# Three host-unrolled head loops of an attention stage written as hardware loops on ScalarE, VectorE and TensorE

## The chip, the cores and the metric

The kernel is a Bass program for one core of a Trainium2 chip. Each engine (TensorE = PE, VectorE = DVE, ScalarE = ACT, GpSimd = POOL, SyncE = SP) has an instruction stream of its own, written by hand, and the streams meet only in semaphores. The metric is the device time of one execution in microseconds.

## The reference, cut to what matters

Two transformer blocks run one after the other on 1024 tokens of width 1024. The first has a short convolution, dilated attention and an FFN. The second puts 16 meta tokens ahead (1040 rows), runs two attention branches A and B over them, merges these with gates, and ends in an expert-choice FFN of 16 experts. The change lies in branch A, the differential attention of 8 heads. Each head has two score maps (m = 0, 1) of width 64 and one value matrix of width 128:

```python
A_HEADS, A_HEAD_DIM = 8, 64
def diff_attention(q, k, v, pos, slopes, lam):
    # q, k: [B, L, H, 2, d]; v: [B, L, H, 2d]
    scale = A_HEAD_DIM ** -0.5
    k_meta = pos < N_META
    def block(qb, pb):
        qp = pb[0]
        s = jnp.einsum('bqhmd,bkhmd->bhmqk', qb, k).astype(jnp.float32) * scale
        dist = jnp.abs(qp[:, None] - pos[None, :]).astype(jnp.float32)
        dist = jnp.where((qp[:, None] < N_META) | k_meta[None, :], 0.0, dist)
        s = s - slopes[None, :, None, None, None] * dist
        p = jax.nn.softmax(s, axis=-1)
        w = p[:, :, 0] - lam * p[:, :, 1]
        return jnp.einsum('bhqk,bkhe->bqhe', w.astype(v.dtype), v)
    return sweep_queries(block, q, pos[None])
```

q, k and v of each head are columns of one projection of the normed rows, h @ w_in.

## The kernel before, in words

All arithmetic is float32. A projection (`project_split`, L513) splits both operands into a rounded part and a remainder and adds three products, so each weight tile of 1024x128 takes three passes on PE. SP loads the tiles one after the other into two buffers, POOL splits them (L540).

Branch A goes head by head. A head has nine query tiles, `t` = 0 to 8: eight of 128 rows and one of 16 (the meta rows). For each tile PE makes the scores of tile `t + 1` (`scores`, L2050), DVE adds the bias and finds the row extremum for both maps (`scores`, L1668), ACT takes both exponentials (`exp`, L1374), DVE combines the two maps into one (`combine`, L1684), PE transposes the result (`turn_probs`, L511), ACT copies the transposes out of PSUM (`take_pt_meta`, `take_pt`, L1382 and L1387), and PE multiplies them with the values (`values`, L2083 and L2084); ACT scales the product into `o_tok` (`result`, L1393). Between these pieces PE projects q, k and v of the next head, one ninth per tile in two halves (`unit`, L2019, 24 matmuls a tile), and ACT and DVE take them out of PSUM (L1351, L1360, L1631, L1635). At tile 5 and at the last tile PE and DVE also make the scores of the 16 meta keys for the next head (`meta_scores`, L2032, L1644, L1648).

The functions `head(h, odd)` of ACT (L1405 on), DVE and PE write one head each. Two heads make a pair because the buffers alternate with the parity of the head. Head 0 and head 7 are written apart. Heads 1 to 6 are three pairs, written in `for i in range((HEADS - 2) // 2)` on ACT (L1443), DVE (L1718) and PE (L2136); with HEADS = 8 this is Python's own loop over i = 0, 1, 2, so the program holds all six heads in a row, and every wait compares with a constant. POOL (L1266) already has a hardware loop over the same pairs. Other stages have hardware loops (`Fori`) on all engines: the first block's attention (L1002 on PE, L820 on DVE, L679 on ACT), the gates and branches (L2190), the first three heads of each group in branch B (L2309; its fourth head is written apart, with the same function), and the experts (L2419).

What sets the order around the change is the written order alone. At the border between two heads PE has: the values of tile 7, the meta scores of the next head, then the scores of tile 1 of the next head, the transpose of its values' meta rows (L511 on `vTa`), and the next projection unit.

Of the kernel before, what the change touches and what calls it, by code (L numbers as in the profile page):

```python
# [38 lines left out]
HEADS = 8  # L39
# [78 lines left out]
def build(nc, A, out):  # L118

    ctx = ExitStack()  # L120
    with ctx:
# [1045 lines left out]
        with nc.Block() as block:  # L1167
# [170 lines left out]
            def _(act):  # L1338
# [64 lines left out]
                def head(h, odd, first=False, last=False):  # L1403

                    for t in range(NT + 1):  # L1405
                        par = (odd + t) % 2
                        before = (h, t - 2) if t >= 2 else None if first else (h - 1, NT + 1 + t - 2)
                        if before:
                            result(*before)
                        if t == 0:  # L1410
                            act.wait_ge(S["aa_v"], 3 * h + 1)
                            act.activation(Va_meta[odd][0:META, :], bank(6, P, 0, META), ACT.Copy).then_inc(S["aa_vs"], 1)
                        after = (h, odd, t + 1) if t < NT else None if last else (h + 1, 1 - odd, 0)
                        if after:
                            exp(after[0], (after[1] + after[2]) % 2, after[2], 0)
                        if before:
                            square(*before)
                        take_pt_meta(h, par, t, first and t < 2)
                        if after:
                            exp(after[0], (after[1] + after[2]) % 2, after[2], 1)  # L1420
                        take_pt(h, par, t)
                        if not last:
                            kind, c = UNITS[t]
                            unit_done(h + 1, kind, c)
                            take_unit(h + 1, 1 - odd, kind, c, WEAVE)
                        if t == 0:
                            for n in range(2):
                                act.wait_ge(S["aa_v"], 3 * h + n + 2)
                                act.activation(Va[:, 4 * n:4 * n + 4, :], bank(5 + n).rearrange("p (t n) -> p t n", n=P), ACT.Copy).then_inc(S["aa_vs"], 1)
# [10 lines left out]
                for c in range(3):  # L1440
                    take_values(0, c, (6, 7, 4)[c])
                head(0, 0, first=True)
                for i in range((HEADS - 2) // 2):  # L1443
                    head(2 * i + 1, 1)
                    head(2 * i + 2, 0)
                head(HEADS - 1, 1, last=True)
# [161 lines left out]
            def _(dve):  # L1608
# [82 lines left out]
                def head(h, odd, first=False, last=False):  # L1691

                    for t in range(NT + 1):
                        if t < NT:
                            attend(h, (odd + t + 1) % 2, t + 1, first)
                        elif not last:
                            attend(h + 1, 1 - odd, 0)
                        if last:
                            continue
                        kind, c = UNITS[t]  # L1700
                        if kind == "k":
                            lower_keys(h + 1, 1 - odd, c, WEAVE)
                        elif kind == "q":
                            lower_queries(h + 1, c)
                        if t == 5:
                            meta_scores(h + 1, True)
                        elif t == NT:
                            meta_scores(h + 1, False)
# [6 lines left out]
                attend(0, 0, 0, True)  # L1715
                meta_scores(0, False)
                head(0, 0, first=True)
                for i in range((HEADS - 2) // 2):  # L1718
                    head(2 * i + 1, 1)
                    head(2 * i + 2, 0)  # L1720
                head(HEADS - 1, 1, last=True)
# [29 lines left out]
                for g in range(KV):  # L1751
                    z0 = g * (GROUP + 1)
                    for n in range(GROUP + 1):
                        i = z0 + n
# [245 lines left out]
            def _(pe):  # L2000
# [85 lines left out]
                def head(h, odd, first=False):  # L2086

                    for t in range(NT + 1):
                        if t < NT:
                            scores(h, odd, t + 1, first)  # L2090
                        else:
                            scores(h + 1, 1 - odd, 0)
                        if t == 0:
                            pe.wait_ge(S["aa_vf"], 3 * h + 3)
                            if not first:
                                pe.wait_ge(S["aa_pt"], 18 * h)
                            turn(bank(6, P, 0, META), vTa[:, T1:T2]).then_inc(S["aa_v"], 1)
                        kind, c = UNITS[t]
                        unit(h + 1, 1 - odd, kind, c, 0)
                        turn_probs(h, (odd + t) % 2, t, first)  # L2100
                        unit(h + 1, 1 - odd, kind, c, 1)
                        if t >= 1:
                            values(h, odd, t - 1, 18 * h + 2 * t + 1)
                        else:
                            if not first:
                                values(h - 1, 1 - odd, NT, 18 * h + 1)
                            pe.wait_ge(S["aa_pt"], 18 * h + 2)
                            turn_values(h)
                        if t == 5:
                            pe.wait_ge(S["aa_pt"], 18 * h + 2 * t + 2)  # L2110
                            meta_scores(h + 1, True)
                        elif t == NT:
                            pe.wait_ge(S["aa_pt"], 18 * h + 2 * t + 2)
                            meta_scores(h + 1, False)
# [18 lines left out]
                pe.wait_ge(S["aa_qs"], 3)  # L2133
                project_split(pe, 0, A0 + 2, (6, 7, 4), CH, u2_hi, u2_lo, start_first)
                head(0, 0, first=True)
                for i in range((HEADS - 2) // 2):  # L2136
                    head(2 * i + 1, 1)
                    head(2 * i + 2, 0)

# [58 lines left out]
                for g in range(KV):  # L2198
# [19 lines left out]
                    for n in range(GROUP + 1):  # L2218
                        i = z0 + n
# [259 lines left out]
```

## Time and profile before

| what | us |
|---|---|
| median of 3 runs (3660.18 to 3663.93) | 3662.32 |
| the profiled execution | 3663.93 |
| span in its trace | 3661.9 |
| PE busy | 3405.9 (93%) |
| DVE busy | 1439.4 (39%) |
| ACT busy | 990.7 (27%) |
| POOL busy | 796.2 (22%) |

The heads of branch A take the stretch from about 1455 to 2078 us of the span; the six heads of the three pairs lie from about 1532 to 2011 us. "PEclk" is the granted clock of TensorE as a share of full speed. DMA queues of the kind "instruction" carry the program itself. A q behind an engine's name (PEldq, ACTq) marks its sequencer: waits, register operations and branches, which are not counted as busy. PE's matmuls and weight loads (PEld) share one sequencer.

### The profile page before, as it was taken

Reading aid. Unit: us, or ns where it says so; the run is one execution under the profiler, and the core shown is the slowest. Engines: PE = TensorE matmul, PEld = TensorE weight load, DVE = VectorE, ACT = ScalarE, POOL = GpSimd, SP = SyncE. Lnnn points to the kernel's source line nnn. Section 1 sums busy time; section 2 is a strip of 40 time slices with the busy share of each in tenths; the row PEclk is TensorE's granted clock in tenths of the full one; section 3 lists DMA queues with packets and bytes.
Section 4 is the critical chain, followed back from the end, with each engine's and each line's share of the span. In section 5 each row is a group of like instructions: output and inputs, shape, how many; then the busy total and the mean of one; then the engine's idle time right before and its main releaser. Section 6 shows DMA issues by size and latency. Waiting matters only on the chain.

```text
span 3661.9 us, 52597 instructions
## 1 busy us (share of the span) xinstructions
PE 3405.9 (93%) x20742; PEld 2971.6 (81%) x20742; DVE 1439.4 (39%) x2414; ACT 990.7 (27%) x1763; POOL 796.2 (22%) x515
## 2 busy tenths in 40 slices
PE   8999989999999998999999799999999999879996
PEld 6667767788887887999998689888877999669996
DVE  3453362100002545666666420555465134432222
ACT  3321240100001213555555410244244210301011
POOL 3112103333332333121222032200100122112221
PEclk9899989999999999999999999999999999889998
DMA  4001012111112112000000011200000121458886
GB/s 150 18 29 34 23 58 89 38 52 46 46 46 93 46 52 88 18 24 18 19 18 24 6 40 40 94 1 12 24 1 12 47 93 64 162 193 295 298 297 237
DMA packets 69667, 269.54 MB, mean 74 GB/s; under 512 B 8832, under 2 KB 9984, under 8 KB 68784
## 3 DMA queue, kind: packets, MB, share of 16 engines
q1 hardware_dynamic: 62336, 228.81, 18.1%
q0 software_dynamic: 5632, 17.04, 1.9%
q10 hardware_dynamic: 1584, 22.07, 1.5%
q8 instruction: 82, 1.34, 0.2%
q14 instruction: 33, 0.27, 0.0%
HBM read 229.55 MB, written 38.34 MB: 73 GB/s over the span
## 4 chain that ended last, share of the span: by engine, by line
PE 54%; DVE 3%; issue 2%; ACT 1%; DMA 0%; POOL 0%; DVEq 0%; ACTq 0%; POOLq 0%; SPq 0%
PE PS L523 17%; PE PS L2019 7%; PE PS L2397 6%; PE PS L511 5%; PE PS L2285 4%; PE PS L2083 4%; PE PS L2405 3%; PE PS L2050 3%; PE PS L2264 2%; PE PS L2208 1%; PE PS L2213 0%; PE PS L2251 0%; PE PS L2084 0%; PE PS L2286 0%; DVE EB L1829 0%
## 5 line engine op out<-in xcount | busy, mean ns | idle before, releaser
L523 PE MATMUL PS<-u_hi,w_hi 128*128 128x512 f32 (+1 forms) x1960 | 547.8, 371 | 28.5 <-DVE u_lo L477 11.5
L545 POOL CAST w_hi<-ring 128x1024 fp32r<-128x1024 f32 x174 | 182.6, 1049 | 1743.3 <-PE PS L523 1318.4
L523 PE MATMUL PS<-u_lo,w_hi 128*128 128x512 f32 (+1 forms) x1960 | 546.5, 370 | 0.0
L523 PE MATMUL PS<-u_hi,w_lo 128*128 128x512 f32 (+1 forms) x1960 | 543.8, 369 | 0.0
L547 POOL TENSOR_TENSOR w_lo<-ring,w_hi 128x1024 fp32r<-128x1024 f32 x174 | 435.0, 2500 | 14.0
L523 PEld LDWEIGHTS PS<-u_hi,w_hi 128*128 128x128 f32 x1960 | 355.6, 190 | 97.9 <-issue 34.0
L523 PEld LDWEIGHTS PS<-u_hi,w_lo 128*128 128x128 f32 x1960 | 356.6, 189 | 57.0
L523 PEld LDWEIGHTS PS<-u_lo,w_hi 128*128 128x128 f32 x1960 | 357.5, 190 | 51.5
L1374 ACT ACTIVATE EA<-EA,small_sb 128x1040 f32<-128x1040 f32 x144 | 166.6, 1157 | 207.7 <-DVE small_sb L1668 207.7
L928 DVE TENSOR_TENSOR hid<-sq,PS 128x1024 f32 x22 | 26.9, 1221 | 457.9 <-PE PS L523 457.9
L1668 DVE CUSTOM_DVE_ANT_0 EA<-PS,biasH,low_a 128x1024 f32<-128x1024 f32 x128 | 163.6, 1278 | 65.3 <-PE PS L2050 65.3
L2019 PE MATMUL PS<-u_hi,w_hi 128*128 128x348 f32 x504 | 173.5, 344 | 0.0
L2285 PEld LDWEIGHTS PS<-PTb,Vb 128*128 128x128 f32 x1152 | 135.9, 193 | 41.5 <-ACT PTb L1533 41.0
L2285 PE MATMUL PS<-PTb,Vb 128*128 128x128 f32 (+1 forms) x1152 | 147.8, 281 | 21.0 <-ACT PTb L1533 21.0
L2083 PE MATMUL PS<-Va,PTa 128*128 128x128 f32 (+1 forms) x1152 | 145.9, 282 | 18.6 <-ACT PTa L1382 18.6
L2019 PE MATMUL PS<-u_lo,w_hi 128*128 128x348 f32 x504 | 162.1, 322 | 0.0
L2019 PE MATMUL PS<-u_hi,w_lo 128*128 128x348 f32 x504 | 161.9, 321 | 0.0
L2083 PEld LDWEIGHTS PS<-Va,PTa 128*128 128x128 f32 (+1 forms) x1152 | 138.1, 186 | 24.0 <-ACT PTa L1382 20.5
L934 DVE TENSOR_TENSOR hid_lo<-hid,hid_hi 128x1024 fp32r<-128x1024 f32 x44 | 94.0, 2176 | 123.3 <-ACT hid_hi L765 123.3
L2397 PE MATMUL PS<-xsT,w_gate_sb 128*128 128x130 f32 x1024 | 128.3, 278 | 1.7 <-DVE xsT L1965 0.7
L1684 DVE SCALAR_TENSOR_TENSOR EA<-EA,small_sb,EA 128x1040 f32<-128x1040 f32 (+1 forms) x72 | 127.1, 1765 | 2.5
L2405 PE MATMUL PS<-hidT,w_down_sb 128*128 128x130 f32 x1024 | 118.8, 276 | 9.8 <-issue 6.8
(351 smaller groups left out, 5726.6 us busy)
## 6 DMA issues: line engine op xcount, KB each, us to landing
ring<-in_stream SPq DMA_DIRECT2D x174, 512.0 KB, 3.5
w_gate_sb<-in_w_gate SPq DMA_DIRECT2D x64, 512.0 KB, 5.7
w_up_sb<-in_w_up SPq DMA_DIRECT2D x64, 512.0 KB, 6.5
w_down_sb<-in_w_down SPq DMA_DIRECT2D x64, 512.0 KB
x_keep<-xT ACTq DMA_DIRECT2D x2, 4176.0 KB, 13.0
xT<-x_keep ACTq DMA_DIRECT2D x1, 4176.0 KB, 12.8
x2T<-x_keep ACTq DMA_DIRECT2D x1, 4176.0 KB, 14.3
x_keep<-x2T SPq DMA_DIRECT2D x1, 4176.0 KB, 13.7
```

What stands on the lines that cost most here:

```text
L511: return nc.tensor.transpose(out, in_, eye[0:k, 0:k])
L523: last = mm(bank(to_bank, width), w[j][:, c, :], src[:, c, b * width:(b + 1) * width], start=(c == 0 and k == 0), stop=(c == KD - 1 and k ...
L545: pool.tensor_copy(w_hi[j][:, :, :], w_raw[j][:, :, :]).then_inc(S["w_rounded"], 1)
L547: pool.tensor_tensor(w_lo[j][:, :, :], w_raw[j][:, :, :], w_hi[j][:, :, :], ALU.subtract).then_inc(S["w_split"], 1)
L1374: act.activation(e[0:m, :], e[0:m, :], ACT.Exp, scale=-1.0, bias=small[0:m, 8 + 2 * par + k:9 + 2 * par + k], accum_out=small[0:m, 12 + 2 ...
L1668: dve.tensor_tensor_reduce(e[0:m, 0:T1], wide(2 * k, T1, m), bias, -1.0, low_a[0:m, t, k:k + 1], ALU.add, ALU.min, low).then_inc(S["aa_max ...
L1684: dve.scalar_tensor_tensor(EA[par][0:m, :], EA2[0:m, :], c2, EA[par][0:m, :], ALU.mult, ALU.add).then_inc(S["aa_c"], 1)
L2019: last = mm(bank(WEAVE, CH), w[slot][:, d, :], src[:, d, columns_of(c)], start=(d == 0 and k == 0), stop=(d == KD - 1 and k == 2))
L2083: mm(bank(7, P, 0, m), PTa[par][:, j, 0:m], Va[:, j, :], start=(j == 0), stop=False)
L2285: mm(bank(7, m), Vb[:, i, :], PTb[t % 2][:, i, 0:m], start=(i == 0), stop=False)
L2397: last = mm(bank(b + 2 * (j % 2), CAP), w[:, j, c, :], xsT[:, c, :], start=(c == 0), stop=(c == KD - 1))
L2405: last = mm(bank(b, CAP, (c % 3) * CAP), w_down[:, j, c * P:(c + 1) * P], hidT[:, j, :], start=(j == 0), stop=(j == EK - 1))
```

## The change

The three Python loops become hardware loops over the same pairs. The program then holds two heads instead of six in each of the three streams, a register holds i, and what depended on i (semaphore counts to wait for, columns of `o_tok` and `ss2`) is worked out from it at run time. POOL and SP are the same instruction for instruction.

```diff
@@ ScalarE, L1440
                 head(0, 0, first=True)
-                for i in range((HEADS - 2) // 2):
+                with act.Fori(0, (HEADS - 2) // 2) as i:
                     head(2 * i + 1, 1)
                     head(2 * i + 2, 0)
                 head(HEADS - 1, 1, last=True)
@@ VectorE, L1715
-                for i in range((HEADS - 2) // 2):
+                with dve.Fori(0, (HEADS - 2) // 2) as i:
                     head(2 * i + 1, 1)
                     head(2 * i + 2, 0)
                 head(HEADS - 1, 1, last=True)
@@ TensorE, L2133
-                for i in range((HEADS - 2) // 2):
+                with pe.Fori(0, (HEADS - 2) // 2) as i:
                     head(2 * i + 1, 1)
                     head(2 * i + 2, 0)
```

Counted in the two built programs, one pair on PE had 1,008 matmuls and their waits, and the body of the loop now has the same and 88 instructions more that set registers (75 REGISTER_ALU, 13 ISA). On DVE a body adds 104 REGISTER_ALU and some 13 ISA, on ACT 79 REGISTER_ALU and 48 ISA.

TensorE, the border between heads 2 and 3 as the program before has it (L2083 and L2084 values, L2032 meta scores, L2050 scores of the next tile, L511 a transpose, L2019 the projection unit):

```order
L2083 MATMUL PS<-Va,PTa_140 128x128 x8
L2084 MATMUL PS<-Va_meta_134,PTa_140 128x128
L2032 MATMUL PS<-kmeta,qTa 128x32 x3
L2032 MATMUL PS<-kmeta,qTa 16x32
L2050 MATMUL PS<-ka_hi_125,qa_hi 128x512 x4
L2050 MATMUL PS<-ka_lo_126,qa_hi 128x512 x4
L2050 MATMUL PS<-ka_hi_125,qa_lo 128x512 x4
L511 MATMUL PS<-eye_sb,vTa 16x128
```

TensorE, the same place in the program after, the end of the loop's body:

```order
L2083 MATMUL PS<-Va,PTa_140 128x128 x8
L2084 MATMUL PS<-Va_meta_134,PTa_140 128x128
L2113 REGISTER_ALU
L2032 MATMUL PS<-kmeta,qTa 128x32 x3
L2032 MATMUL PS<-kmeta,qTa 16x32
L2136 REGISTER_ALU
L2136 COMPARE_AND_BRANCH
```

The matmuls keep their order. What followed in the next row is now reached by a branch back to the start of the body, taken twice (after heads 2 and 4), and not taken after head 6.

VectorE, the end of the loop's body in the program after (L1644 and L1648 take the meta scores; L1665 and L1668, which follow in time, stand at the body's start or, after the last round, behind the branch):

```order
L1644 TENSOR_SCALAR meta_a<-PS 128x96
L1644 TENSOR_SCALAR meta_a<-PS 16x32
L1648 TENSOR_REDUCE low_a<-meta_a 128x6
L1648 TENSOR_REDUCE low_a<-meta_a 16x2
L1718 REGISTER_ALU
L1718 COMPARE_AND_BRANCH
```

Nothing is reordered here either; the two last rows are new, and register operations stand ahead of most waits inside the body.

## Rows read from the trace of the kernel before

**Rows 1.** Busy us by engine over heads 1 to 6, one head a row.
```profile
core 0: us, PE busy (x) PEld busy (x) DVE busy (x) ACT busy (x) POOL busy (x), PEclk, DMA share, GB/s
1533.00:1613.00 80.00, 80.00 (x598) 72.19 (x594) 53.05 (x105) 43.00 (x96) 17.50 (x7) 1.00 0.07 21
sum 480.00, PE 480.00 PEld 433.05 DVE 318.01 ACT 257.97 POOL 105.01; mean PE 80.00 PEld 72.18 DVE 53.00 ACT 42.99 POOL 17.50
```
**Rows 2.** DMA queues (packets, MB), first over 1534 to 2014 us, then over 160 to 515.
```profile
q8 instruction: 28, 0.46, 0.4%
q14 instruction: 12, 0.10, 0.1%
...
q1 hardware_dynamic: 2592, 9.44, 8.9%
```
**Rows 3.** One round of PE's loop L1002, busy us and instructions.
```profile
279.80:398.60 118.80, 110.52 (x571) 85.35 (x570) 49.95 (x102) 30.05 (x57) 20.57 (x12) 0.97 0.09 26
```
**Rows 4.** Timeline at the border of heads 2 and 3: start us, us, engine, what.
```profile
1690.80 0.92 PE L2032 MATMUL PS<-kmeta,qTa 128*128 128x32 f32 x8
1691.65 0.73 PE L2050 MATMUL PS<-ka_hi,qa_hi 64*128 64x512 f32 x4
1693.24 0.28 PE L511 MATMUL PS<-eye_sb,vTa 128*16 128x128 f32 x1
...
1700.75 0.51 DVE L1631 TENSOR_TENSOR ka_lo<-PS,ka_hi 128x348 fp32r<-128x348 f32 x1
...
1702.93 0.19 PEld L2019 LDWEIGHTS PS<-u_hi,w_hi 128*128 128x128 f32 x1 [0.36 <-issue]
```
**Rows 5.** PE's sequencer there: lines L506 and L2096, first and last start.
```profile
L506 PEldq EVENT_SEMAPHORE  x1: 51/51/51, 1689.9 to 1689.9; - x1
...
L2096 PEldq EVENT_SEMAPHORE  x1: 51/51/51, 1691.0 to 1691.0; - x1
```
**Rows 6.** PE's sequencer at the loop L2190: ns min/median/max of each kind.
```profile
L2190 PEldq ALU_OP  x6: 32/32/32, 2147.5 to 2262.0; - x6
L2190 PEldq COMPARE_BRANCH  x6: 76/208/208, 2147.6 to 2262.1; - x6
```
**Rows 7.** ACT at the start of the second block; then DMA queues, 1420.85 to 1421.0 us.
```profile
L1431 ACTq EVENT_SEMAPHORE  x1: 38/38/38, 1419.3 to 1419.3; - x1
...
L1351 ACT ACTIVATE ka_hi<-PS x3: 457/460/468, 1424.1 to 1424.8; 128x348 fp32r<-128x348 f32 x3
...
q14 instruction: 2, 0.02, 25.7%
```
**Rows 8.** What PE waited for, 2012 to 2080 us, then 2120 to 2130, then 2290 to 2380.
```profile
PE PS L2083 <- ACT PTa L1382: 18.6, 8, 2.3
...
PE PS L523 <- DVE oa_lo L1734: 1.7, 1, 1.7
...
PE PS L523 <- issue: 4.2, 3, 1.4
```
**Rows 9.** Busy us and granted clock of short stretches after such waits.
```profile
2126.00:2130.00 4.00, 4.00 (x16) 4.00 (x17) 0.00 (x0) 0.00 (x0) 0.00 (x0) 0.57 0.00 0
2027.00:2031.00 4.00, 4.00 (x20) 3.88 (x22) 1.88 (x5) 2.00 (x3) 0.00 (x0) 0.57 0.00 0
2042.00:2064.00 22.00, 15.00 (x121) 12.30 (x119) 13.55 (x31) 12.69 (x27) 0.00 (x0) 1.00 0.00 1
2316.00:2320.00 4.00, 2.58 (x16) 2.46 (x16) 3.70 (x2) 3.23 (x4) 0.10 (x1) 1.00 0.34 135
```
**Rows 10.** Chain of branch B: first two rows in the loop L2309, last two written apart.
```profile
2430.80 2.05 PE PS L2285 x16
2435.31 2.05 PE PS L2285 x16
...
2571.73 2.05 PE PS L2285 x16
2576.25 2.05 PE PS L2285 x16
```

## The prediction

> **What bounds the kernel now.** I read the page first (PE is busy 93% of the span), then the busy times of the six heads one by one. In each stretch of 80 us PE is busy for 80.00 us at full clock, while DVE is busy 53 and ACT 43 [rows 1]. So in this stage nothing but PE's own work counts: a faster DVE or ACT brings nothing, and a slower one costs only what goes beyond its slack. No matmul goes away with the change. It can gain nothing here that the trace shows, and whatever it does to the time it does by starving PE.
>
> Next the two things that the change touches: how PE's sequencer stands to PE, and how the program itself gets in. At the border of heads 2 and 3 the sequencer handles the wait L2096 at 1691.0 [rows 5]. That wait stands ahead of the transpose of vTa, which starts at 1693.24 [rows 4], so the sequencer is 2.2 us ahead. The new branch stands between L2032 and L2050. The semaphore step ahead of the last, 16-row piece of L2032 is handled at 1689.9 [rows 5], and only one small piece follows it, so the branch would be handled at about 1690.1. The first L2050 starts at 1691.65 [rows 4]: the lead at the branch is 1.55 us.
>
> The code arrives in pieces. Over the six heads q8 brings 28 packets and q14 brings 12 [rows 2]. 0.46 MB over 28 is 16 KB, and PE runs about 1,192 recorded instructions a head (598 + 594 [rows 1]), 7,150 in all, or 255 a packet; so q8 is PE's code, 64 bytes an instruction. q14 (8 KB a packet) then is that of DVE and ACT: 12 packets x 128 = 1,536, against 6 x (105 + 96) = 1,206 recorded and their waits.
>
> **The change part by part.**
>
> *Register operations, 88 a pair on PE, about 120 each on DVE and ACT.* One is 32 ns on PE, and the loop's branch 208 ns when taken and 76 when not [rows 6]. From rows: a PE tile of 8.6 us gets five, with their handling perhaps 0.1 us each, against a lead of 1.5 to 2 us. The nearest direct evidence is branch B, where the same function runs in a loop for three heads and apart for the fourth. PE waits for its neighbours there, so delays would show. The step from one L2285 to the next is 4.51 us in the loop and 4.52 apart from it [rows 10]. Cost: 0, hidden behind PE's queue; without that cover 0.1 us x 88 x 3 = 26 us, the upper bound.
>
> *The branch back, if its target is at hand.* 208 ns plus register steps, under 0.5 us, against a lead of 1.55: cost 0, two times.
>
> *The branch back, if its target is not at hand.* The body on PE holds 2 x 1,192 recorded instructions, some 45 waits and 88 register operations: about 2,520, which is 161 KB or ten packets. On DVE it is about 385 instructions (24 KB), on ACT about 355 (22 KB), three packets each. The largest loop in the trace is L1002, with 571 + 570 and its waits, about 1,220 instructions or 78 KB [rows 3]. In 355 us of its rounds not one instruction packet moves: the second stretch of [rows 2] has q1 alone. So PE keeps at least 78 KB. Whether it keeps 161 KB no row shows. I take it that it does not: straight code is fetched steadily though nothing returns to it, and the body is twice the largest loop kept.
>
> The Trainium skill says the same outright: "Advanced Engine Details and Errata", section ISA Cache, gives TensorE 128 KB and the others 32 KB. By that PE misses at each branch back and DVE and ACT stand at the edge. Its "only 2 cache lines" of 256 instructions would have made L1002 fetch in each round; [rows 2] show that it did not.
>
> What a miss costs is bounded by two rows. At the start of the second block ACT's sequencer has its last event at 1419.3 and then nothing until 1424.1, and the two q14 packets start only at about 1420.9 [rows 7]. If one of them is ACT's, which I read from the count of ACT's instructions and which the row does not name, 1.6 us pass from the request to the first byte. A q8 packet itself takes 0.4% of 16 engines over 480 us, divided by 28: 1.1 us [rows 2]. Together 2.7 us. From 1690.3 the code is there at 1693.0; PE is out of work at 1691.65, so it idles 1.3 us, with the restart about 1.5. Lower end 0 (the request comes early enough). Upper end: the next piece is asked for only after the first has landed and is needed at once, 2 x 2.7 - 1.55 = 3.9 us.
>
> *The clock after such an idle.* In the tail of this stage PE waits eight times for 2.3 us [rows 8]. After some of them the clock falls (0.57 over 4 us), after others it stays at 1.00 [rows 9]. After the wait of 1.7 us it fell to 0.57 of the 2.4 GHz level in the mean, part of it at 1.2 GHz; after one of 1.4 us it stayed [rows 8, 9]. A fall loses (1 - 0.57) x 4 = 1.7 us. For an idle of 1.5 us I take half of that, 0.85; bounds 0 and 3.4, two such falls.
>
> *DVE and ACT at the same border.* If they miss too, they stand still for 1.6 us and a shorter packet, about 2.1. PE first needs DVE's L1631 (1700.75 + 0.51 = 1701.26) at 1702.93 [rows 4]: slack 1.67 us, and 1.5 more when PE has stopped as well. So DVE costs 0 beside PE's own idle, and 0.4 an edge if PE alone finds its code. ACT has over 3 us, the same answer.
>
> *Entering and leaving.* The jump into the body goes to the next address and the last branch is not taken (76 ns): 0.
>
> *Sum.* Two branches back x (1.5 + 0.85) = 4.7 us. PE is the bound before and behind, so nothing gives it back. On the profiled execution 3663.93 becomes 3668.6. That execution lies 1.6 us above the median of 3662.32, so I predict 3667.0.
>
> **The rivals.**
>
> *Nothing is exposed* (the code memory holds the body, or the request runs ahead). For it: loops of 78 KB are kept without a packet [rows 2, 3]. Against it: 161 KB is twice that. Time: 0 to 1 us more, 3662.3 to 3663.3.
>
> *The misses chain and the clock falls, the slower side.* Place: PE's first matmuls L2050 behind the branch. A branch to code that is away stops the sequencer, it refills piece by piece, PE idles 3.9 us, and an idle that long brings two falls of the clock, which lose 3.4. Price 2 x 7.3 = 14.6 us, time 3677. It decides from a loss of 3.65 us an edge on (7.3 in all), for instance an idle of 2.3 us, at which the trace has falls [rows 9], and one fall of 1.7. For it: nothing in the trace shows a taken branch to absent code, so 2.7 us is a guess from a straight start. The Trainium skill, "Runtime: NRT & Kernel Launch", section Instruction fetch mechanics, calls such a branch an ifetch stall and gives no time for it.
>
> *Register operations reach PE.* In the 16-row tiles, where matmuls are short, the lead is smaller. At most 26 us, as above; a third of it would be 9 us, 3671. Against it: [rows 10], and the loop L1002, full of such waits.
>
> *Faster.* A gain would have to come from fewer code packets, but the body is fetched again in each round if it does not fit, and PE has no idle time to give up [rows 1].
>
> **How the numbers follow.** A measurement of this kernel tells about 0.2%, 7.3 us, from no change. Forecast (PE misses, 2 to 7 us): 0.47. Nothing exposed: 0.22. Chained misses with the clock, 8 to 15 us: 0.24. Register operations: 0.04. Faster by something unseen: 0.03. So same is 0.47 + 0.22 = 0.69, slower 0.24 + 0.04 = 0.28, faster 0.03. The range starts just under the median, 3661.5, and reaches to the price of the chained misses, 3677; outside lie the register rival's far end, the far end of the third case and half of the first and last cases' spread. The likeliest case alone spans 3664.3 to 3669.5.
>
> **What would show it.** q8 still brings about 28 packets over the six heads, one of them right at each border 2/3 and 4/5. PE is idle there for 1 to 2 us before L2050, with "issue" as the reason, and not at the borders 1/2, 3/4 and 5/6. The granted clock falls behind one of the two or neither. All other stretches of 80 us have PE busy for 80.00. DVE and ACT may stop at the same borders without PE waiting for them. If no idle time stands before L2050 and q8 falls to some ten packets, the body was kept and the step "not at hand" is wrong. If PE is busy under 80.00 us between the borders, the step on register operations is wrong. If the idle is 3 us or more, my 2.7 us was.

## The result, and the profile of the changed kernel

The changed kernel took 3689.90 us in the median of 19 runs (3669.39 to 3699.55), the kernel before 3664.95 us in 19 runs (3660.18 to 3670.13). The ratio is 1.0057, interval [1.004, 1.0075]: slower by more than the 0.2% that tells it from no change. The prediction was 3667.0 us, range 3661.5 to 3677.0, with "same" as the likeliest outcome; the median lies outside the range, on the slower side.

The times of the changed kernel fall into two groups: seven between 3669.4 and 3674.1, one at 3679.0, and eleven between 3689.4 and 3699.6. The kernel before has one group. The mean granted clock of an execution goes with this: 0.962 or 0.963 in the seven short ones, 0.955 to 0.958 in the eleven long ones. The profiled execution took 3672.89 us (span 3671.1) and is one of the short ones, so it shows only part of the loss. The profile of a repeat, below, shows the rest.

The page, first block and DMA queues, against 3405.9 us of PE, 1439.4 of DVE and 990.7 of ACT before:

```profile
PE 3408.7 (93%) x20742; PEld 2974.6 (81%) x20742; DVE 1439.2 (39%) x2414; ACT 991.6 (27%) x1763; POOL 796.4 (22%) x515
...
q8 instruction: 88, 1.44, 0.2%
q14 instruction: 48, 0.39, 0.0%
```

The engines do the same work. What is new is idle time and more code packets (82 and 33 before), though the program has become shorter. The two queues of code over the heads (1534 to 2022 us), against 28 and 12 packets in [rows 2], and then over 1690 to 1700 us alone, behind the first taken branch, where the kernel before has one packet on q8 and none on q14:

```profile
q8 instruction: 34, 0.56, 0.5%
q14 instruction: 26, 0.21, 0.1%
...
q8 instruction: 3, 0.05, 2.1%
q14 instruction: 3, 0.02, 0.8%
```

The loop's branch on PE's, DVE's and ACT's sequencer (ns minimum, median, maximum; then the first and the last start in us):

```profile
L2136 PEldq COMPARE_BRANCH  x3: 83/4067/4211, 1690.2 to 2018.8; - x3
...
L1718 DVEq COMPARE_BRANCH  x3: 60/63/68, 1694.4 to 2023.0; - x3
...
L1443 ACTq COMPARE_BRANCH  x3: 40/45/50, 1689.0 to 2017.6; - x3
```

The taken branch on PE lasts 4.07 and 4.21 us, where the loop in [rows 6] has 208 ns. It is handled at 1690.2 us; the prediction had 1690.1. The records of DVE and ACT put the time elsewhere: their branch row is short and the stop lies behind it. On DVE it shows as idle time ahead of L1665, the first operation at the top of the body (in the kernel before, L1665 starts 0.4 us behind L1648 there):

```profile
1693.95 0.33 DVE L1648 TENSOR_REDUCE low_a<-meta_a 128x6 f32<-128x96 f32 x2
1697.78 0.17 DVE L1665 COPY EA<-meta_a 128x16 f32<-128x16 f32 x1 [3.50 <-issue]
```

PE at the border of heads 2 and 3, to be held against [rows 4], and all that PE waited for from 1440 to 2010 us:

```profile
1690.77 0.92 PE L2032 MATMUL PS<-kmeta,qTa 128*128 128x32 f32 x8
...
1694.46 0.73 PE L2050 MATMUL PS<-ka_hi,qa_hi 64*128 64x512 f32 x4 [2.77 <-issue]
```

```profile
PE PS L2050 <- issue: 5.7, 2, 2.9
PE PS L511 <- ACT PTa L1387: 0.6, 1, 0.6
```

L2032 starts within 0.03 us of its time before, and L2050 comes 2.81 us later than its 1691.65. The two waits hold 5.7 us, one at each border where the branch is taken. Behind each the clock falls. Busy us and granted clock (the first number after POOL's busy time and count) of a stretch between two borders, of one right behind the first border, and of one behind the second:

```profile
1703.00:1783.00 80.00, 80.00 (x597) 72.28 (x595) 52.77 (x104) 42.48 (x95) 17.50 (x7) 1.00 0.07 21
...
1695.80:1699.10 3.30, 3.30 (x15) 2.88 (x12) 1.22 (x2) 0.27 (x1) 0.00 (x0) 0.50 0.01 2
1859.70:1862.90 3.20, 3.20 (x15) 2.48 (x12) 1.03 (x2) 0.27 (x1) 0.00 (x0) 0.50 0.04 10
```

Between the borders PE is busy for 80.00 of 80 us, so the register operations cost nothing. Behind each idle of 2.8 us the clock stands at the lower level (0.50 is 1.2 GHz) for some 3.4 us, which loses half of that, 1.7 us. The stage loses 5.7 + 3.4 = 9.1 us, and the tail behind the heads starts 9 us later. The tail wins some back: the first branch of the loop behind it, L2190, is handled at 2154.1 us against 2147.6 [rows 6], 6.5 us later. PE waits as long in the tail as before (18.8 us against 18.6), but the mean clock over its 68 us is 0.92 and not 0.87. In the repeat below the tail takes as long as in the kernel before, so the gain belongs to this execution and not to the change. Up to the end of branch A the program is therefore 6.5 us late in this execution.

At its end it is 9.2 us late (a span of 3671.1 against 3661.9). The other 2.7 us are lost in branch B. Its first loop's branches, before and changed:

```profile
L2309 PEldq COMPARE_BRANCH  x6: 76/208/215, 2443.5 to 2829.8; - x6
...
L2309 PEldq COMPARE_BRANCH  x6: 76/208/217, 2450.0 to 2839.1; - x6
```

The first is 6.5 us late, the last 9.3. Between them the clock is at the lower level for 6.8 us more than in the kernel before, which at half speed is 3.4 us.

### The profile page after: what moved, and what is told of

It reads as the page before. It is cut to its first block, busy times and chain, and to the rows that moved or that the text cites. A ratio compares the mean times of both kernels' runs of the same rounds, so it can differ in the third digit from the quotient of the medians.

```text
span 3671.1 us, 53565 instructions
## 1 busy us (share of the span) xinstructions
PE 3408.7 (93%) x20742; PEld 2974.6 (81%) x20742; DVE 1439.2 (39%) x2414; ACT 991.6 (27%) x1763; POOL 796.4 (22%) x515
## 4 chain that ended last, share of the span: by engine, by line
PE 53%; DVE 4%; issue 2%; ACT 1%; DMA 0%; POOL 0%; DVEq 0%; ACTq 0%; POOLq 0%; SPq 0%
PE PS L523 17%; PE PS L2397 6%; PE PS L2019 6%; PE PS L511 5%; PE PS L2285 4%; PE PS L2083 3%; PE PS L2405 3%; PE PS L2050 3%; PE PS L2264 2%; PE PS L2208 1%; PE PS L2251 0%; PE PS L2213 0%; PE PS L2286 0%; PE PS L2084 0%; DVE EB L1829 0%
## 5 line engine op out<-in xcount | busy, mean ns | idle before, releaser
L1374 ACT ACTIVATE EA<-EA,small_sb 128x1040 f32<-128x1040 f32 x144 | 166.9, 1159 | 205.0 <-DVE small_sb L1668 204.4
L1668 DVE CUSTOM_DVE_ANT_0 EA<-PS,biasH,low_a 128x1024 f32<-128x1024 f32 x128 | 163.6, 1278 | 64.8 <-PE PS L2050 64.3
L2019 PE MATMUL PS<-u_hi,w_hi 128*128 128x348 f32 x504 | 174.6, 346 | 0.0
L2019 PE MATMUL PS<-u_lo,w_hi 128*128 128x348 f32 x504 | 163.0, 323 | 0.0
L2019 PE MATMUL PS<-u_hi,w_lo 128*128 128x348 f32 x504 | 162.7, 323 | 0.0
L2083 PE MATMUL PS<-Va,PTa 128*128 128x128 f32 (+1 forms) x1152 | 143.9, 279 | 18.8 <-ACT PTa L1382 18.8
L2083 PEld LDWEIGHTS PS<-Va,PTa 128*128 128x128 f32 (+1 forms) x1152 | 135.9, 183 | 24.2 <-ACT PTa L1382 21.1
```

The source lines that it names most:

```text
L1374: act.activation(e[0:m, :], e[0:m, :], ACT.Exp, scale=-1.0, bias=small[0:m, 8 + 2 * par + k:9 + 2 * par + k], accum_out=small[0:m, 12 + 2 ...
L1668: dve.tensor_tensor_reduce(e[0:m, 0:T1], wide(2 * k, T1, m), bias, -1.0, low_a[0:m, t, k:k + 1], ALU.add, ALU.min, low).then_inc(S["aa_max ...
L2019: last = mm(bank(WEAVE, CH), w[slot][:, d, :], src[:, d, columns_of(c)], start=(d == 0 and k == 0), stop=(d == KD - 1 and k == 2))
L2083: mm(bank(7, P, 0, m), PTa[par][:, j, 0:m], Va[:, j, :], start=(j == 0), stop=False)
```

## The experiments

All ratios are against the kernel before, run on the same chip beside the kernels named.

**The same kernel again.** No edit. My theory after the result was that the misses (a taken branch whose target the engine does not have at hand) cost some 9 us in every execution, and that the clock takes the rest in some of them, behind the borders.

> The changed kernel once more, to see how its executions spread and, if the profiled one is long, where the 26 us lie. Theory (idle and clock): executions fall in two groups, about +6 to +9 us and +25 to +34 us over the kernel before; in a long one the granted clock stays at the lower level for some 20 us or more behind one or both of the borders 2/3 and 4/5, and nowhere else is there more loss. Rival (waits lost elsewhere): a long one shows idle time of PE spread over the loop, at full clock.

Measured: 3680.59 us in 10 runs, 3665.35 before in 22; ratio 1.0046 [1.0027, 1.0064]. Five runs lie between 3671.2 and 3675.7, one at 3685.5, and four between 3693.5 and 3696.0. The profiled execution was a long one, 3693.50 us (span 3691.7), 20.6 us above the short profile. First its branch on PE, then two stretches of branch B, and then the branches of branch B's two loops:

```profile
L2136 PEldq COMPARE_BRANCH  x3: 83/3707/3871, 1688.1 to 2016.0; - x3
...
2535.10:2558.80 23.70, 23.15 (x92) 20.55 (x93) 7.87 (x21) 3.82 (x9) 0.00 (x0) 0.50 0.02 6
2838.90:2862.60 23.70, 22.82 (x91) 20.26 (x92) 7.64 (x21) 3.83 (x9) 0.00 (x0) 0.50 0.03 11
...
L2309 PEldq COMPARE_BRANCH  x6: 76/208/215, 2449.7 to 2854.0; - x6
L2314 PEldq COMPARE_BRANCH  x4: 76/208/211, 2924.5 to 2993.2; - x4
```

The same rows of the short execution (its L2309 stands above):

```profile
2535.10:2558.80 23.70, 22.57 (x155) 20.13 (x156) 10.86 (x30) 8.25 (x16) 0.00 (x0) 0.93 0.03 11
...
L2314 PEldq COMPARE_BRANCH  x4: 76/208/211, 2904.3 to 2973.1; - x4
```

Read the start times. At 2450 us both executions are level (2449.7 and 2450.0; the long one had entered branch A 2 us earlier and lost 2 us more there). The short one reaches the last branch of L2309, in the second group, at 2839.1 and the long one at 2854.0. At L2314 it is 2924.5 against 2904.3. So the 20 us lie in branch B and not behind the borders. The clock rows say how: at 2535.10 and again at 2838.90 TensorE runs at 1.2 GHz for 23.7 us without a break. PE is busy all the while (23.15 of 23.7), but it gets through 92 matmuls where the short execution has 155. A low stretch loses half its length, 12 us here, against 1.7 us for the stretch of 3.4 us that the short execution has at the same place: about 10 us more each. The mechanism of my theory (the clock) was right and its place wrong.

Both executions have the same waits of PE from 2525 to 2540 us:

```profile
PE PS L2285 <- ACT PTb L1533: 2.5, 2, 1.3
PE PS L511 <- DVE EB L1829: 2.1, 1, 2.1
```

PE's transposes (L511) wait 2.07 us there for DVE's division of the probabilities (L1829), and the clock falls behind that wait, for 3.4 us in the short execution and for 23.9 in the long one. The kernel before has the same wait and a fall of 3.4 us behind it (2528.8 to 2532.2 us of its span).

**The loop on PE alone.** `for` becomes `with pe.Fori` at L2136; DVE and ACT stay unrolled.

> Only PE has the hardware loop; DVE and ACT stay unrolled. Theory (PE's code is fetched again and that alone counts): two idles of 2.7 to 2.9 us, median as of the changed kernel, +9 to +30 us, with the same two groups. Rival (the stops of DVE and ACT at the same border are what PE waits for or what makes the long executions): under +5 us and one group.

Measured: 3673.89 us in 12 runs (3667.26 to 3692.14); ratio 1.0026 [1.0014, 1.0039]. Ten of the twelve lie at 3681.2 or below.

```profile
L2136 PEldq COMPARE_BRANCH  x3: 83/3487/3887, 1691.9 to 2018.0; - x3
...
PE PS L2050 <- issue: 4.7, 2, 2.6
```

PE misses by itself. Its branch takes 3.49 and 3.89 us and exposes 2.55 us at the first border and 2.14 at the second. The clock falls behind the second idle and not behind the longer first one. I had expected the two groups and a median as of the changed kernel. The median is 8.5 us above the kernel before and not 25, and only two of twelve (3685.5 and 3692.1) come near the long group, so the loop on PE alone brings few of the long executions.

**The loops on DVE and ACT, PE unrolled.**

```diff
-                for i in range((HEADS - 2) // 2):        # ScalarE, L1443
+                with act.Fori(0, (HEADS - 2) // 2) as i:
-                for i in range((HEADS - 2) // 2):        # VectorE, L1718
+                with dve.Fori(0, (HEADS - 2) // 2) as i:
```

> DVE and ACT have the hardware loops, PE is unrolled. Theory: DVE has 1.67 us of slack and a miss of about 2.1 us, so 0 to 1 us at a border, 0 to +2 us in all, no long executions. Rival: +5 us or more.

Measured: 3694.35 us in 6 runs (3677.89 to 3697.73, five at 3691.3 or above); ratio 1.0069 [1.0054, 1.0085]. I had expected next to nothing. PE's waits, 1690 to 1900 us:

```profile
PE PS L2083 <- ACT PTa L1382: 6.7, 2, 3.4
```

PE waits 3.4 us at each border for ACT's copy of the transposes. So one of the two other engines stops long enough to reach PE, which my sum had at nothing. The next two runs tell which. The profile is a long one (3697.73 us) and has the stretch in branch B too, and a second one from 2843.5 us on:

```profile
2539.80:2563.40 23.60, 22.99 (x92) 20.40 (x93) 7.80 (x21) 3.72 (x9) 0.00 (x0) 0.50 0.02 8
```

**The loop on DVE alone, and the loop on ACT alone.**

> Only DVE has the hardware loop. In the run with loops on DVE and ACT, DVE's branch took 3.5 us and PE waited 3.4 us for L2083 at each of the borders 2/3 and 4/5. Theory (DVE's late scores hold the exponentials of tile 1, and ACT's copies L1382 of tile 0 stand behind these in ACT's order): PE waits twice for 3 to 3.4 us at L2083 here too, and the attention stage is 9 to 11 us longer. Rival (ACT's own miss makes that wait): PE has no idle at L2083.

> Only ACT has the hardware loop. Theory: ACT's branch takes 2.5 us, and its slack at the border is over 3 us, so PE idles nowhere in heads 1 to 6 and the median is within 2 us of the kernel before. Rival (ACT's miss counts): two waits of PE of over 1 us, +5 us or more.

Measured: DVE alone 3697.52 us (3697.10, 3697.94, 3674.37, 3699.12), ratio 1.007 [1.0043, 1.0097]. ACT alone 3664.74 us in 10 runs (3658.80 to 3671.38), ratio 1.0003 [0.9993, 1.0013], and PE waits for nothing between 1690 and 1900 us. The chain with DVE alone, at the border of heads 2 and 3:

```profile
1695.48 0.33 DVE L1648 TENSOR_REDUCE low_a<-meta_a 128x6 f32<-128x96 f32 x2
1699.50 0.17 DVE L1665 COPY EA<-meta_a 128x16 f32<-128x16 f32 x1 [3.68 <-issue]
...
1701.10 1.16 ACT L1374 ACTIVATE EA<-EA,small_sb 128x1040 f32<-128x1040 f32 x1 [5.80 <-DVE small_sb L1668]
...
1702.68 0.27 ACT L1382 ACTIVATE PTa<-PS 16x128 f32<-16x128 f32 x1
...
1702.99 3.24 PE L2083 MATMUL PS<-Va,PTa 128*16 128x128 f32 x15 [3.19 <-ACT PTa L1382]
```

DVE idles 3.68 us behind its branch. The extremum of tile 1 (L1668) comes late, ACT's exponential L1374 waits for it, and ACT's copy L1382 of the tile before, whose transposes (L511) end at 1697.9 us, stands behind that exponential in ACT's stream. PE waits for the copy. The prediction looked only at L1631 as PE's next need of DVE [rows 4]. The nearer one goes through ACT's order. In the changed kernel this wait is hidden, because PE stops at the same border itself: from 1440 to 2010 us the only wait for ACT is 0.6 us. ACT's loop is free. DVE's loop alone also gives long executions, three of four, and its profile (3697.10 us) has both stretches of branch B; with the loop on PE alone they were rare.

**Idle time at the borders of the kernel before, without a loop.** This tells a cost of code fetching from a cost of idle time.

```diff
                     head(2 * i + 2, 0)
+                    if i < 2:
+                        for _ in range(45):
+                            seen(pe)
```

> No loop at all: the kernel before, with 45 semaphore steps more on PE's sequencer at each of the borders 2/3 and 4/5, so that PE runs dry there for about as long as behind the branch (45 x 0.093 = 4.2 us less the lead of 1.55: 2.6 us). Theory (an idle of that length is what costs, through the clock, whatever makes it): +5 us of idle and the same two groups, median +9 to +30 us. Rival (the long executions come from fetching code or from the loop): +5 to +9 us, in one group.

Measured: 3679.16 us in 6 runs (3673.06 to 3680.32); ratio 1.0032 [1.002, 1.0044]. The edit was larger than meant: a step of `seen`, which adds 1 to a semaphore, took PE's sequencer 0.15 us, so PE idles 5.2 us a border in place of the planned 2.6:

```profile
PE PS L2050 <- issue: 10.4, 2, 5.2
```

The granted clock behind the second of them (us, PE busy, clock, DMA share, GB/s):

```profile
1867.00:1870.00 3.00, 2.99 (x14) 0.50 0.00 0
```

At both borders it stands at the lower level for 6.8 us, beginning before the wait ends, and the stage lost 15.4 us. With no branch and no miss the clock falls as well, so idle time alone is enough for it. The median is smaller than the changed kernel's although more is lost in the stage, and none of the six executions is among the long ones. A larger delay does not by itself bring them.

**Half a microsecond on DVE in branch B, without a loop.** If the long stretches come from how branch B's own wait lies, a small shift there must bring them in the kernel before. Five steps of `seen` (0.47 us together) go ahead of one row extremum at the start of branch B's first group:

```diff
-                    def scores(j, t):
+                    def scores(j, t, late=0):
...
-                        seen(dve)
+                        for _ in range(1 + late):
+                            seen(dve)
...
-                    scores(0, 1)
+                    scores(0, 1, 0 if g else 5)
```

> The kernel before, with no loop added, and 5 semaphore steps more on DVE (5 x 0.093 = 0.47 us) ahead of one row extremum at the start of branch B's first group. Theory (the 20 us of the long executions are lost in branch B, where the clock after PE's longest wait falls for 3 or for 24 us depending on how that wait lies in time against the clock's changes, so a shift of half a us decides): executions of +10 us or +20 us appear, with the clock low for some 24 us near 2530 us, although nothing else is changed. Rival (the long executions need the code misses of the loops): +0.5 us, all executions between 3660 and 3671.

Measured: 3683.71 us in 9 runs against 3664.95 in 20; ratio 1.0037 [1.0018, 1.0057]. Four runs lie between 3662.2 and 3670.4, and five between 3683.7 and 3689.6 (none of the 20 executions of the kernel before does). So half a microsecond made the two groups, in a program with no loop in branch A. The median moved by 19 us because the long group happens to hold five of nine. The long executions themselves have no profile. The profiled one was short (3668.19 us); behind the first group's wait it shows no fall, behind the second group's one of 6.8 us (from 2820.2):

```profile
2535.00:2559.00 24.00, 23.63 (x171) 20.71 (x171) 13.60 (x34) 12.10 (x22) 0.00 (x0) 1.00 0.00 1
```

**Eight such steps (0.74 us).** The same edit with 8 for 5.

> The kernel before with 8 semaphore steps (0.74 us) on DVE at the start of branch B, where 5 of them made five of nine executions some 20 us longer. Theory (how PE's 2.1 us wait lies against the clock's changes decides): long executions of +20 to +28 us again, and if the profiled one is long, the clock stays low for some 24 us behind that wait, with no code packet and no idle of PE ahead of it. Rival (the long executions are lost elsewhere): a long one shows its extra time outside branch B.

Measured: 3677.31 us in 10 runs (four from 3665.3 to 3669.7, five from 3677.0 to 3678.2, one at 3684.2), against 3665.65; ratio 1.0022 [1.0008, 1.0036]. The profiled one was long by some 10 us (3677.64) and shows one stretch of 24 us, behind the second group's wait. The same stretch in the kernel before follows it:

```profile
2822.70:2846.30 23.60, 22.34 (x91) 19.69 (x90) 7.17 (x21) 4.01 (x8) 0.00 (x0) 0.50 0.05 18
```

```profile
2822.70:2846.30 23.60, 23.28 (x170) 20.39 (x169) 12.60 (x33) 9.79 (x18) 0.00 (x0) 1.00 0.00 1
```

91 matmuls against 170 in the same time. PE's only long wait near it is again one of 2.1 us for DVE's division (L1830 in that program). So an unrolled program has the long stretch as well, once in this execution; two of them make the 20 us of the changed kernel. The larger delay moved the median by 12 us and the smaller by 19. The intervals of the two ratios overlap, so these runs do not order the two delays.

**Twenty-two such steps (2.05 us) in the changed kernel.** If the place of the wait decides, a larger shift could lead out of it again.

> The changed kernel with 22 such steps (2.05 us) at the same place. Theory: the two waits of branch B move out of the place where the clock stays low, no execution is longer than +14 us, and the median falls from +20 to about +10 us although 2 us of waiting are added. Rival: the same two groups, 2 us later.

Measured: 3684.57 us in 6 runs (3680.72 to 3690.61); ratio 1.0057 [1.0044, 1.0069]. All six lie between or at the edge of the two groups. Four stretches of the profiled one (3684.01 us), the clock again ahead of the last two columns:

```profile
2539.00:2546.00 7.00, 5.74 (x29) 0.52 0.25 75
2594.00:2601.00 7.00, 6.73 (x26) 0.52 0.00 0
2700.00:2707.00 7.00, 7.00 (x24) 0.53 0.00 0
2836.00:2843.00 7.00, 5.74 (x30) 0.52 0.21 75
```

In place of two stretches of 24 us at 1.2 GHz there are several of some 7 us, two of them behind the two waits of branch B. I had expected the median near the short group; it was no cure.

**A smaller body on PE.** Is it the size of the body that makes the branch miss? PE's loop alone is kept (DVE and ACT unrolled). The projection unit issues 2 of its 24 matmuls and the third score product is gone, so this kernel leaves work out and its time (3607.8 us) says nothing. The body is then about 1,580 instructions, 101 KB, in place of 161.

```diff
-                    for d in range(half * HALF, (half + 1) * HALF):
-                        for k, (w, src) in enumerate(((w_hi, u2_hi), (w_hi, u2_lo), (w_lo, u2_hi))):
...
+                    for d in (half * (KD - 1),):
+                        last = mm(bank(WEAVE, CH), w_hi[slot][:, d, :], u2_hi[:, d, columns_of(c)], start=(d == 0), stop=(d == KD - 1))
...
-                    for n, (q, keys) in enumerate(((qa_hi, ka_hi[odd]), (qa_hi, ka_lo[odd]), (qa_lo, ka_hi[odd]))):
+                    for n, (q, keys) in enumerate(((qa_hi, ka_hi[odd]), (qa_hi, ka_lo[odd]))):
```

> PE alone has the hardware loop, and its body is made small by leaving work out: of the 24 matmuls of a projection unit 2 stay, and the third product of the scores is gone in all heads of this stage. The body then holds about 1,580 instructions (101 KB, six to seven packets) instead of 2,520 (161 KB). Theory (a body that is larger than what PE keeps is fetched again): no q8 packet falls in the second and third round, the branch takes 0.2 us and PE has no wait for issue ahead of L2050. Rival (any jump that far back, or past the next packets, is a miss): the branch takes 3.5 to 4.2 us as before and q8 keeps bringing packets.

The branch, and the DMA queues from 1660 to 1940 us:

```profile
L2135 PEldq COMPARE_BRANCH  x3: 76/215/215, 1662.8 to 1939.6; - x3
...
q1 hardware_dynamic: 1728, 6.29, 7.3%
...
q14 instruction: 8, 0.07, 0.1%
```

The branch takes 215 ns, no q8 packet moves in 280 us of rounds, and PE does not wait at the border. PE keeps a body of 101 KB and not one of 161 KB.

**One branch back in place of two.** Heads 1 and 2 are written apart on all three engines, and the loops run over the two pairs that are left:

```diff
+                head(1, 1)
+                head(2, 0)
-                with pe.Fori(0, (HEADS - 2) // 2) as i:
+                with pe.Fori(1, (HEADS - 2) // 2) as i:
```

> All three engines have the loop, but heads 1 and 2 are written apart, so that the loop has two rounds and one branch back (border 4/5). Theory: one idle of 2.4 to 2.9 us and one fall of the clock, so the attention stage is 4 to 5 us longer than before instead of 9 to 10; what branch B adds (0 to 20 us) hangs on its place in time and not on the number of branches, so the median lies anywhere between +4 and +25. Rival (all the loss scales with the branches): +9 to +13 in the median.

Measured: 3671.63 us in 11 runs (eight from 3669.4 to 3672.3, then 3679.9, 3680.8 and 3692.5); ratio 1.0026 [1.0012, 1.004].

```profile
PE PS L2054 <- issue: 2.5, 1, 2.5
```

One taken branch, one idle. With half the branches the excess over the kernel before is 6.0 us in the median against 25 and 15 us with two. By their times most of these executions were short in branch B, as the profiled one was; I had left the median open between +4 and +25.

**The same wait in all profiles.** The twelve profiles with all the work in them hold PE's wait for DVE's division twice each, once in each group of branch B, and it is always 2.06 to 2.08 us long. How long the clock stays low behind it goes with how long after its end the clock falls:

| the clock falls, us after the wait's end | it stays at 1.2 GHz for | waits |
|---|---|---|
| -0.05 to 0.75 | 6.8 us | 6 |
| 0.96 to 1.83 | 23.9 us | 7 |
| 1.94 to 2.27 | 3.4 us | 6 |
| no fall behind it | 0 | 5 |

The three long profiles (the repeat, the loops on DVE and ACT, and DVE alone) have 1.83 and 1.49, 1.73 and 1.48, 1.70 and 1.47 us; the changed kernel's short one has 1.95 and 1.94. Its wait ends at 2533.47 us and its clock falls at 2535.42. In the repeat these are 2533.19 and 2535.02. A tenth of a microsecond lies between 1.7 us lost and 12. This was read from the profiles afterwards. No run set this distance on purpose, and what sets it in a single execution is not known.

No kernel here beats the one before. The loop on ACT alone costs nothing.

## Why the prediction was wrong, step by step

- **Register operations, cost 0: right.** PE is busy 80.00 of 80 us between borders.
- **Entering and leaving, cost 0: right.** The branch that is not taken takes 83 ns.
- **The body is not at hand on PE: right.** 34 packets in place of 28, a stop at both taken branches, and a body of 101 KB without one. The Trainium skill's 128 KB for TensorE ("Advanced Engine Details and Errata", ISA Cache) lies between 101 and 161 KB, and no run here places the limit more closely. The other figure of that section of the Trainium skill, two cache lines, does not hold for PE here: the body of 101 KB is some six pieces of 16 KB.
- **What a miss costs on PE, 2.7 us and 1.5 exposed: too small.** It took 3.49 to 4.21 us at all nine taken branches (five profiles) and exposed 2.1 to 2.9. The lead of 1.55 us was nearly right: in the changed kernel's profile 4.07 + 4.21 us of branches exposed 5.7, which is 1.3 us hidden at each. The working took the price of a straight start, 1.6 + 1.1 us, for that of a jump to absent code; the exposed term, 1.5 us, was mis-sized by 1.35 us a border in that profile.
- **The clock behind it, 0.85 us a border: too small.** Both idles brought a fall, 3.4 us at the lower level, 1.7 us lost each; over the five profiles eight of nine idles did. The rival had said so: "an idle of 2.3 us, at which the trace has falls".
- **DVE's miss costs 0: wrong by itself, hidden in the sum.** Its sequencer stands still for 2.8 to 3.5 us behind the branch and not for 2.1, and PE needs DVE sooner than at L1631, by way of ACT's order. Alone it costs PE 3.2 us a border; in the changed kernel PE stops at the same time. ACT's 0 was right.
- **"PE is the bound before and behind, so nothing gives it back": the step that failed.** Up to the end of branch A the measured sum is 9.1 in place of 4.7, of which the tail gives 2.6 back: 6.5 us on 3662.32 are 3668.8, inside the range and just within 0.2% (in the repeat, where the tail gives nothing back, it is some 2 us more). The sum put everything behind that at nothing. Branch B, whose wait comes some 500 us behind the second taken branch, is bound by latency: [rows 10] came from that stage and were read only for the register operations. Behind its wait of 2.1 us for DVE the clock stays at full speed in some executions, and falls for 3.4, 6.8 or 24 us in others; two stretches of 24 make 20 us. By their times and clocks, eleven of 19 executions of the changed kernel have them, and none of the kernel before, which has the same wait. The profile of the short execution alone would not have told this.

The rival "the misses chain and the clock falls" (3677) had the right kind of cost, at 2 x 7.3 us. It measured 2 x 4.6 us where it was put, and the larger part of the median's loss came from elsewhere.

**How firmly this is shown.** Shown: the miss on PE and its dependence on the body's size; the clock's fall behind idle time without a loop; the 20 us in branch B, by two profiles of one kernel; that half a microsecond on DVE is enough to bring the two groups to an unrolled program; and that the length of a low stretch goes with its distance from the wait, without an exception in 24 waits. Argued only: that it is the shift in time that the changed kernel brings to branch B, by whatever way, that plays the part of those five steps. A rival is untested: each of these edits also changes the number of instructions ahead of branch B, and with it where the pieces of code begin there; no run changed the one without the other. It can bear only on how often the long stretches come, since one and the same program has executions with and without them. Open: what sets the distance between wait and fall in a single execution; why PE's loop alone brings few long executions and DVE's alone many; why DVE's sequencer stands for 2.8 to 3.5 us where ACT's stands for 2.4 to 2.9 (in the changed kernel ACT is at the branch at 1689.04 and has its next event at 1691.56); and what caused the other falls of 7 us in the run with 22 steps.

## What to carry to other kernels

Count the bytes between a hardware loop's branch and its target. If they exceed what a loop in the same trace is seen to keep, price a taken branch as a fetch (here 3.5 to 4.2 us on PE and 2.8 to 3.5 on DVE), compare it with how far the sequencer is ahead, and follow each in-order neighbour to see who waits. And do not end the sum where the change ends: look for later stages in which PE waits about 2 us for another engine, because there a shift of less than a microsecond can decide how long the clock stays low. With times in two groups, take a profile of each before explaining either.

## What the runs showed of the hardware that was not expected

- A taken branch to absent code holds PE's sequencer for 3.49 to 4.21 us (nine branches in five profiles); with the code at hand it takes 0.21.
- At the half clock PE looks almost fully busy: 22.3 to 23.2 of some 23.7 us, with 91 or 92 matmuls in place of 155 to 170. Only the granted clock and the count of instructions tell.
- A stretch at 1.2 GHz lasted 3.4 us at an idle of 2.8 us, 6.8 at one of 5.2, and 3.4, 6.8 or 23.9 at one of 2.1: the longest stretch came with the shortest idle. Which of the three it was went with how long after the idle the clock fell.
- A semaphore step took PE's sequencer 0.15 us (45 of them: a wait of 5.2 us behind a lead of some 1.5) and DVE's 0.09.
- A loop of about 385 instructions (24 KB) on DVE already misses, while one of about 230 (15 KB) in the first block brings no packet [rows 2]. On ACT a loop of 22 KB misses too (its sequencer stands for 2.4 to 2.9 us), but nobody waits for it.
